# RWKV mixer on one core: chunk loop reordered with four-block products, values centred on entry, head sums and spreads in 32-column and 32-row blocks, two key tiles side by side

## The reference

```python
def rwkv7_mixer(h, ...):
    dx = shift(h) - h
    proj = h @ w_in + dx @ (w_in * mu_cols)
    r, k, v, g, w_lo, a_lo = _split(proj, RW_WIDTHS)
    ...
    def step(S, inp):
        sa = jnp.einsum('bhvk,bhk->bhv', S, -kk_t)
        S = S * w_t[:, :, None, :] + sa[..., None] * b_t[:, :, None, :] + v_t[..., None] * k_t[:, :, None, :]
        return S, jnp.einsum('bhvk,bhk->bhv', S, r_t)
    ...
    y = head_norm(y, ln_g, ln_b, RW_GN_EPS)
    y = y + jnp.sum(r * k * r_k.astype(F32), axis=-1, keepdims=True) * v
    y = y.reshape(B, T, RW_WIDTH) * jax.nn.silu(g.astype(F32))
    return y.astype(h.dtype) @ w_out
```

## Time and profile before

| what | value |
|---|---|
| median of 3 runs | 1509.1 us (1506.23 to 1509.64) |
| profiled execution: its own time | 1511.26 us |
| its span (first to last instruction) | 1509.5 us |
| mean granted TensorE clock | 0.974 |
| PE busy | 1400.7 us, 93% |
| DVE busy | 724.3 us, 48% |
| ACT busy | 449.7 us, 30% |
| POOL busy | 49.9 us, 3% |

### The profile page before, as it was taken

One profiled execution on the slowest core, in us unless ns is written; L12 is line 12 of the kernel. 1 busy time (PEld: TensorE's weight loads), 2 busy tenths in 40 slices (PEclk: granted clock), 3 DMA queues, 4 the chain that ended last, 5 costly groups with the idle time before them and its releaser, 6 DMA issues. The chain is left out here.

```text
span 1509.5 us, 23200 instructions
## 1 busy us (share of the span) xinstructions
PE 1400.7 (93%) x9939; PEld 733.5 (49%) x9939; DVE 724.3 (48%) x1418; ACT 449.7 (30%) x978; POOL 49.9 (3%) x48
## 2 busy tenths in 40 slices
PE   4999999888998999879899989898999999888997
PEld 2444444588534444464344446544444444588533
DVE  5784757644543002171245023525784757744552
ACT  2113262377301011370112052501113252377401
POOL 0000230100000000000000000000000230100000
PEclk8999999999999999999899989998999999999999
DMA  6222222010400222101222221114221222001301
GB/s 202 70 70 56 70 71 70 1 33 30 170 0 0 65 75 78 62 2 56 58 70 84 69 56 29 56 56 132 70 70 56 70 63 77 2 13 50 115 15 56
DMA packets 111183, 92.43 MB, mean 61 GB/s; under 512 B 5020, under 2 KB 99524, under 8 KB 110568
## 3 DMA queue, kind: packets, MB, share of 16 engines
q1 hardware_dynamic: 110504, 88.85, 19.3%
q10 hardware_dynamic: 576, 2.10, 0.4%
HBM read 84.64 MB, written 6.29 MB: 60 GB/s over the span
## 5 line engine op out<-in xcount | busy, mean ns | idle before, releaser
L871 PE MATMUL bank<-arena 128*128 128x512 f32 x1024 | 452.6, 600 | 8.9 <-DVE arena L628 7.5
L871 PEld LDWEIGHTS bank<-arena 128*128 128x128 f32 x1024 | 194.5, 192 | 251.6 <-issue 242.0
L826 PE MATMUL bank<-arena 64*64 64x64 f32 (+2 forms) x6208 | 182.2, 228 | 27.7 <-ACT arena L574 16.2
L826 PEld LDWEIGHTS bank<-arena 64*64 64x64 f32 (+1 forms) x6208 | 161.9, 137 | 60.1 <-issue 32.6
L1192 PE MATMUL bank<-arena 128*128 128x512 f32 x256 | 117.0, 612 | 3.0 <-DVE arena L1152 3.0
L159 ACT ACTIVATE arena<-arena 128x1024 f32<-128x1024 f32 x20 | 21.1, 1055 | 254.1 <-DVE arena L1160 142.5
L1192 PEld LDWEIGHTS bank<-arena 128*128 128x128 f32 x256 | 48.7, 195 | 70.4 <-issue 64.7
L628 DVE SCALAR_TENSOR_TENSOR arena<-arena 128x512 f32<-128x512 f32 x96 | 70.6, 786 | 0.0
L1661 PE MATMUL bank<-arena 128*128 128x512 f32 x160 | 69.0, 592 | 0.0
L1293 PE MATMUL bank<-arena 128*128 128x512 f32 x128 | 57.1, 609 | 1.6 <-PEq L1089 1.6
L2068 PE MATMUL bank<-arena 128*128 128x512 f32 x128 | 55.8, 593 | 0.9 <-DVE arena L2112 0.9
(11 more groups left out here) (231 smaller groups left out, 1640.1 us busy)
## 6 DMA issues: line engine op xcount, KB each, us to landing
arena<-in_rw_w_in SPq DMA_DIRECT2D x66, 512.0 KB, 4.0
arena<-in_ml_w_in SPq DMA_DIRECT2D x24, 512.0 KB, 3.8
arena<-in_sw_w_in SPq DMA_DIRECT2D x20, 512.0 KB, 3.7
arena<-in_rw_w_out SPq DMA_DIRECT2D x16, 512.0 KB, 7.4
spill<-arena SPq DMA_DIRECT2D x2, 2048.0 KB, 8.6
arena<-spill SPq DMA_DIRECT2D x2, 2048.0 KB, 7.7
arena<-in_sw_w_out SPq DMA_DIRECT2D x8, 512.0 KB, 3.6
arena<-in_ml_w_out SPq DMA_DIRECT2D x8, 512.0 KB, 3.5
```

The lines of the kernel that those rows point to most:

```text
L826: mm = lambda out, a, b, start=True, stop=True: nc.tensor.matmul(out, a, b, start=start, stop=stop, skip_group_check=True)
L871: last = nc.tensor.matmul(bank[:, :], slot[:, k, :], mix_at[what][:, k, :], start=k == 0, stop=k == KT - 1)
```

## The change

What it does, in the order of the program:

- stage_load: the 24 rows of parameters come in two groups, one set for the first layer (PE waits for it alone), the rest on SP's and ACT's queues, turned after the first norm tile. ACT takes a Sqrt of a constant first.
- rw_mix, start: the first two key tiles are multiplied side by side, one mixed input at a time (first_two_keys).
- POOL multiplies R*K by r_k as well (one more operation per chunk, between R*K and the scaling of B), and later squares Y of each chunk into L.
- turn_values makes V's transposes as 16 products with 64 columns of the centring matrix, so that V in the loop is centred per head.
- Loop: products_r ahead of solve; outputs issues the S products of both halves first; xu and right_side_values are one function, complete_and_begin, whose matmuls go through all four 64x64 blocks. Entry to the loop: turn_values(0) ahead of the last g tile, x(0) right behind it in banks 2 and 3, the first R products in banks 4 and 5, place_inverse(0) and place_transpose(0) earlier.
- rw_gate_out: no centring, squaring or copying; the sums of squares are four groups of 4 output rows at rows 0, 32, 64, 96 of one bank (cleared to 1.0 by DVE first), the spreads read groups of 4 rows at the same places, in groups of four and then two; the bonus products use the plain head-sum matrix; six bonus multiplies stand ahead of the reciprocal.
- ml_project: the first two u tiles stand ahead of the gate rows.

```diff
+            load_rows(sp, 0, rw[0], loaded)
+            load_rows(sp, 2, rw[1], others_loaded)
...
+            act.wait_ge(zeroed.handle, 1)
+            nc.scalar.activation(m.view(A_SMALL + 41, 1), m.view(A_SMALL + 41, 1), ACT.Sqrt)
+            load_rows(act, 1, sw_ml, others_loaded)
...
+            pe.wait_ge(loaded.handle, 16 * (len(rw[0]) + 1))
+            turn_params(0, m.bank[0], 0).then_inc(turned.handle, 1)
             for a in range(NT):
+                if a == 1:
+                    pe.wait_ge(others_loaded.handle, 16 * (len(rw[1]) + len(sw_ml)))
+                    turn_params(1, m.bank[7], 0)
+                    turn_params(2, m.bank[7], P).then_inc(turned.handle, 1)
                 norm.turn(pe, a)
...
                 nc.gpsimd.tensor_tensor(R[:, :, span(c)], R[:, :, span(c)], K[:, :, c, :], ALU.mult).then_inc(rk_ready.handle, 1)
+                pool.wait_ge(rk_ready.handle, rk_ready.at(c + 1))
+                nc.gpsimd.tensor_tensor(R[:, :, span(c)], R[:, :, span(c)], rk, ALU.mult).then_inc(scaled_rk.handle, 1)
                 nc.gpsimd.tensor_tensor(BB[:, :, c, :], BB[:, :, c, :], epi[c], ALU.mult).then_inc(b_scaled.handle, 1)
...
+            nc.gpsimd.memset(S, 0.0).then_inc(s_cleared.handle, 1)
+            for c in range(NC):
+                pool.wait_ge(y_evac.handle, y_evac.at(2 * c + 2))
+                nc.gpsimd.tensor_tensor(L[:, :, span(c)], KK[:, :, span(c)], KK[:, :, span(c)], ALU.mult)
...
-            for j in range(KT):
+            for j in range(KT - 1):
                 read_tile(place["g", j])
             place_inverse(0)
+            read_tile(place["g", KT - 1])
...
-            for j in range(len(INVERT_UPTO), KT - 1):
+            gate(len(INVERT_UPTO))
+            place_transpose(0)
+            for j in range(len(INVERT_UPTO) + 1, KT):
                 gate(j)
-            place_transpose(0)
-            gate(KT - 1)
-            dve.wait_ge(tile_done.handle, tile_done.at(len(tiles)))
-            nc.vector.memset(S, 0.0)
+            mask_x(0)
             mask_r(0)
-            mask_x(0)
+            complete_u(0)
             place_transpose(1)
...
+            def first_two_keys():
+                slots = []
+                for n in range(2):
+                    m.weights_arrived(pe, n0 + n)
+                    slots.append(m.view(m.slot(n0 + n), KT, P))
+                for k in range(KT):
+                    pe.wait_ge(mixed.handle, mixed.at(k + 1))
+                    for n in range(2):
+                        last = nc.tensor.matmul(tile_bank(n)[:, :], slots[n][:, k, :], mix_at["k"][:, k, :], start=k == 0,
+                                                stop=k == KT - 1)
+                        if k == KT - 1:
+                            last.then_inc(tile_done.handle, 1)
+                slot_used[0] += 2
...
-                        last = nc.tensor.transpose(m.bank[q][LO, P * k:P * k + P], V[:, 4 * q + k, span(c)], ident)
+                        for par, rows in enumerate((HI, LO)):
+                            last = mm(m.bank[q][rows, C * k:C * k + C], V[:, 4 * q + k, span(c)], centre[:, C * par:C * par + C])
...
-            def xu(c):
+            def complete_and_begin(c):
                 banks_23_read()
                 pe.wait_ge(u_placed.handle, u_placed.at(c + 1))
+                if c == 0:
+                    pe.wait_ge(gr_evac.handle, gr_evac.at(2))
                 for g in range(2):
                     pe.wait_ge(xs_ready.handle, xs_ready.at(2 * c + g + 1))
-                    for k in range(4):
-                        p = 4 * g + k
-                        for par, rows in SIDES:
-                            last = mm(m.bank[2 + g][rows, C * k:C * k + C], xs[rows, p, :], tu[c][rows, p, C:P])
-                    last.then_inc(xu_done.handle, 1)
-                given["xu"] = c + 1
-            def right_side_values(c):
-                for g in range(2):
                     pe.wait_ge(v_evac.handle, v_evac.at(2 * c + g + 1))
                     if c >= 1:
                         pe.wait_ge(y_evac.handle, y_evac.at(2 * (c - 1) + g + 1))
                     for k in range(4):
+                        p = 4 * g + k
+                        for par, rows in SIDES:
+                            completed = mm(m.bank[2 + g][rows, C * k:C * k + C], xs[rows, p, :], tu[c][rows, p, C:P])
                         for par, (rows, others) in enumerate(((LO, HI), (HI, LO))):
-                            h = 2 * (4 * g + k) + par
-                            last = mm(m.bank[4 + g][rows, C * k:C * k + C], ga[c][others, h, :], z[c][others, h, :], k == 0, False)
-                    last.then_inc(rhs_begun.handle, 1)
+                            h = 2 * p + par
+                            begun = mm(m.bank[4 + g][rows, C * k:C * k + C], ga[c][others, h, :], z[c][others, h, :], k == 0, False)
+                    completed.then_inc(xu_done.handle, 1)
+                    begun.then_inc(rhs_begun.handle, 1)
+                given["xu"] = c + 1
...
-            for n in range(place["v", 0]):
+            first_two_keys()
+            for n in range(2, place["v", 0]):
                 project(n)
             pe.wait_ge(act_done.handle, act_done.at(place["v", 0]))
             for c in range(NC):
                 project(place["v", c])
                 products_a(c)
-            for n in range(place["g", 0], len(tiles)):
+            for n in range(place["g", 0], len(tiles) - 1):
                 project(n)
             pe.wait_ge(ga_evac.handle, ga_evac.at(2 * NC))
             turn_values(0)
-            pe.wait_ge(t_turned.handle, t_turned.at(1))
+            project(len(tiles) - 1)
+            x(0)
             products_r(0)
-            pe.wait_ge(gated.handle, gated.at(KT))
             turn_bk(0)
-            x(0)
-            right_side_values(0)
-            xu(0)
+            complete_and_begin(0)
+            pe.wait_ge(s_cleared.handle, s_cleared.at(1))
             for c in range(NC):
                 right_side_state(c)
                 if c + 1 < NC:
                     turn_values(c + 1)
+                    products_r(c + 1)
                 solve(c)
                 if c + 1 < NC:
-                    products_r(c + 1)
                     x(c + 1)
                 outputs(c)
                 if c + 1 < NC:
                     turn_bk(c + 1)
-                    xu(c + 1)
-                    right_side_values(c + 1)
+                    complete_and_begin(c + 1)
...
             act.wait_ge(ready.handle, ready.at(1))
-            for j in range(KT):
-                act.wait_ge(centred_done.handle, centred_done.at(j + 1))
-                nc.scalar.activation(sq[:, j, :], m.bank[j][:, :], ACT.Square).then_inc(squared.handle, 1)
+            nc.scalar.activation(m.view(A_SMALL + 41, 1), eps, ACT.Sqrt)
             act.wait_ge(var_done.handle, var_done.at(1))
-            nc.scalar.activation(rstd[0:NH, :], m.bank[0][0:NH, :], ACT.Sqrt, bias=eps[0:NH, :], scale=1.0 / C)\
-                .then_inc(root.handle, 1)
+            nc.scalar.activation(rstd, m.bank[0][:, :], ACT.Sqrt, bias=eps, scale=1.0 / C).then_inc(root.handle, 1)
...
+            nc.vector.memset(eps, 64e-5)
+            nc.vector.memset(m.bank[0][:, :], 1.0).then_inc(ready.handle, 1)
+            for j in range(6):
+                add_bonus(j)
...
+            def spread(js):
+                for j in js:
+                    if j >= 4:
+                        pe.wait_ge(spread_used.handle, spread_used.at(j - 3))
+                for j in js:
+                    nc.tensor.matmul(spread_bank(j)[:, :], pick[group(j), j * P:(j + 1) * P], rstd[group(j), :],
+                                     start=True, stop=True).then_inc(spread_done.handle, 1)
...
-            for j in range(KT):
-                nc.tensor.matmul(m.bank[j][:, :], centre, Y[:, j, :], start=True, stop=True).then_inc(centred_done.handle, 1)
-            pe.wait_ge(centred.handle, centred.at(1))
-            for j in range(KT):
-                pe.wait_ge(squared.handle, squared.at(j + 1))
-                last = nc.tensor.matmul(m.bank[0][0:NH, :], compact(j), sq[:, j, :], start=j == 0, stop=j == KT - 1)
+            for j in range(4):
+                bonus(j)
+            pe.wait_ge(ready.handle, ready.at(1))
+            for i in range(2):
+                for q in range(4):
+                    last = nc.tensor.matmul(m.bank[0][group(q), :], compact(i), sq[:, 4 * i + q, :], start=i == 0, stop=i == 1,
+                                            skip_group_check=True)
             last.then_inc(var_done.handle, 1)
-            for j in range(6):
+            for j in range(4, KT):
                 bonus(j)
             pe.wait_ge(inverse.handle, inverse.at(1))
...
+                if k in (1, 3):
+                    spread(range(k + 3, k + 5))
...
-    tiles = [("gates", 0)] + [("u", j) for j in range(KT)] + [("z", j) for j in range(ML_EARLY_Z)]
```

(1 more changed line is left out.)

146 lines of the change are left out of this document (67 added, 79 removed).

## The result

The changed kernel takes 1475.38 us (median of 4 runs, 1473.26 to 1476.89), beside 1509.37 (4 runs) for the kernel before in the same series: a ratio of 0.9774, 95% interval 0.9757 to 0.979. It is faster by 34 us where 53 were forecast, and lies outside the range of 1444 to 1470. The profiled execution took 1473.26, with a span of 1471.2; against the profiled execution of before, the span fell by 38.3.

A forecast was written before the change was run, and what follows sets the result against it. The prediction took TensorE as busiest, its chunk loop bound by a PE and ACT cycle of 12.37 us. Terms 26.6 + 27.6 - 6.0 - 2.6 + 2.7 + 4.4 = 52.7 off 1511.3 gave 1458.6, hence 1456; range 1444 to 1470.

The forecast's parts named there:

- step (1): Chunk loop: moving the R products from between solve and x to ahead of solve saves 0.95 us per chunk.
- the ring: Chunk loop's repeating cycle of PE and ACT work between reads of right sides: 12.37 us, forecast to become 11.09.
- us_ready: Rival: this wait, ahead of the moved R products, closes the loop, so no gain; must cost 3.8 us per chunk; 2%.
- step (2): Chunk loop: issuing both halves' S products before the first wait removes two matmul mode changes, 0.33 us per chunk.
- the entry: Start of the chunk loop: x(0) right behind the last gate tile, second read of right sides 6.0 us earlier per layer.
- Step (3): Chunk loop: merged complete_and_begin saves 0.9 us of PE per chunk, but off the critical cycle, so no gain in time.
- step 5: Chunk loop: GpSimd squares Y, 1.3 us per chunk, costing nothing there; VectorE ends 0.6 later after the last chunk.
- Ahead of the loop: Before the first products_a: GpSimd's extra multiply delays scaling and VectorE; loss 3.0 us per layer, 6 in both.
- the small covers: Rival: GpSimd's multiply hides and the starts run at full clock; 1447 us; 8%.
- 32-column blocks that do not overlap: Rival, gate stage: 32-row and 32-column blocks run without overlap, 3.4 and 1.7 us more per layer; 1466 us; 8%.
- The half clock in the loop: Rival: the loop falls to half clock, +5.7 us per chunk, slower than before; about 1536 us in all 14; 2%.
- PE as the loop's bound: Rival: PE replaces ACT because the merged stretch is slow, its four blocks served one after the other; 1480 us; 4%.

The follow-up runs named there:

- x_behind_s: Changed kernel with x(c+1) moved behind both halves' S products instead of straight behind solve; 1466.99 us, ratio 0.9727 to the kernel before.
- r_behind_solve: Changed kernel with products_r(c+1) put back between solve and x; 1482.73 us, ratio 0.9826 to the kernel before.
- s_apart: Changed kernel with the S products kept but issued half by half, as before the change; 1480.72 us, ratio 0.9815 to the kernel before.
- rk_in_loop: x_behind_s with GpSimd's multiplies by r_k moved from the v tiles into the loop; 1463.04 us, ratio 0.9684 to the kernel before.
- b_scaled_first: Changed kernel with GpSimd scaling B before it multiplies by r_k; 1472.10 us, ratio 0.9762 to the kernel before.
- params_last: Changed kernel with the second parameter group turned and copied at the end of stage_load; one profiled execution, first key product at 23.82, 2.55 earlier.
- inverse_on_gpsimd: x_behind_s with the inverse's copies for chunks 2 to 7 on GpSimd instead of ScalarE; 1467.80 us, ratio 0.9724 to the kernel before.

## Why the prediction was wrong

**The loop, step (1), failed.** "That takes 0.95 from the ring" took for granted that x could start when solve had been issued. products_r had been the cover of ACT's four value copies: they end 2.25 us behind the start of the read of right sides in the changed kernel's rows, and x needs their banks. What one takes out ahead of a wait must be checked against every semaphore of the instruction that moves up, and I checked only those that products_r itself waits for. I named as a doubt that ACT's chain might hold something that I counted as free, looked for it in the inverse copies, and as rival only with us_ready and a price of 3.8; it was v_evac, at 0.93. Fourteen rings of 0.93 are 13.0 of the 14.4 us that the forecast sum is too high for the profiled execution. x_behind_s shows it by taking the wait away, r_behind_solve by putting the cover back: at full clock its ring is the same.

**The loop, step (2), was right** (0.33 forecast, 0.29 measured in s_apart), and so was the entry: x(0) right behind the last g tile, no idle of 4.41 any more. The first read of right sides came at 298.56, with the v tiles 2.6 later than before, so 0.4 behind its forecast. **Step (3)** was right in that merging lies off the ring; its size was 0.7, not 0.9. Squares on GpSimd (step 5): no row shows anything that waits for them; no run leaves them out.

**Ahead of the loop** the loss was forecast at 6.0 and came to 6.4, at the products named, and rk_in_loop gives all of it back. Both causes stand in the prediction, the order for the first products and the hold on the mixes for the third; it was theory A of b_scaled_first that had only the order. "A whole operation each time" does not hold for the mixes: a third operation of 1.38 beside them cost them 0.79.

**The layer's start** was forecast at -2.6 and measured at -1.4. The step is right in kind: a new idle of 1.15 stands before n2(0), and without the two tiles 1.7 comes back. The size was off since the first layer's key tiles ran less time at half clock (15.41 for them, not 16.2).

**stage_load** was mis-sized, 1.0 for 2.7. PE's first parameters came 2.3 earlier, but VectorE's copy of the second group waits for a transpose that PE makes behind the first norm tile, and the second tile's mean is queued behind that copy (14.99 in VectorE's row; PE's second norm tile at 16.52). params_last shows that this was the rest of it.

**The gate stage** was right to 5%: first output product 14.93 behind the start (14.9 forecast), output part 60.21 (59 to 60). In the second layer the spreads ran at half clock, which cost one of the 1.3 us that are missing. **mLSTM** came out at its forecast: from the end of the norm ahead of it to the first product of its output norm the time fell from 300.5 to 296.1, by 4.4. The other 1.4 of the table's row are no gain of the change: attention has the same code, and its first 128 matmul instructions took 55.17 us for 57.12.

Of the rivals, the small covers did not hold (1.52 idle before the first products_a), and 32-column blocks that do not overlap are refuted by 7.03 against 1.90. The half clock in the loop was given 2% and does not occur in the changed kernel (1.00 from 294.57 to 387.84 and from 1293.87 to 1386.82), but r_behind_solve shows how near it is. PE as the loop's bound came true in inverse_on_gpsimd, through its stream of instructions and not through the four blocks.

## What to carry to other kernels

Before an instruction group is moved off a critical ring, list what became ready while it ran: a group that fills time between two waits is a cover, and the next instruction inherits the wait. The cure is often a different filler (here the S products, which need neither bank nor copy), and the ring's length, read between two like events, shows within one chunk whether it worked, even where the whole time does not. And look where an idle engine's new work stands among the waits of others: the same GpSimd multiply cost 6.4 us beside the v tiles and nothing that can be measured in the loop.
